# Grouped attention in a two-part transformer kernel: first scores inside the last tile of values, two halves of weights made beside late units, first sum of squares behind a column

## The chip, the cores and the metric

The kernel runs on one core of one Trainium2 chip. The metric is the time of one execution on the device in microseconds (us), lower is better; the median of several executions is given. Besides the DMA engines the core has TensorE (PE, matmuls and weight loads), VectorE (DVE), ScalarE (ACT), GpSimd (POOL, idle here) and SyncE (SP, which issues the DMAs). Each engine works through its own instructions in the order written, and they wait for each other through counting semaphores.

## The reference

Two transformer layers (differential attention, then grouped attention, each between two feed-forward halves), followed by two layers of a second kind. The change touches the grouped attention of the second layer, which is computed for the 256 positions of the main sequence (`ctx_out` is false there); keys and values also cover the 256 context positions:

```python
GA_HEAD_DIM = 128; GA_HEADS = 8; GA_KV_HEADS = 2
def gqa_axial_mixer(h, hc, w_in, q_norm, k_norm, w_out, ctx_out):
    q, k, v = project(h)        # one projection, q and k normed per head (rmsnorm over 128)
    qc, kc, vc = project(hc)
    q, k = apply_rope(q, cos, sin), apply_rope(k, cos, sin)
    k_all = jnp.concatenate([kc, k], axis=1)
    v_all = jnp.concatenate([vc, v], axis=1)
    # grouped_attend per block of 128 queries:
    s = jnp.einsum('blhgd,bkhd->bhglk', q, k) * scale
    p = jax.nn.softmax(s, axis=-1)
    o = jnp.einsum('bhglk,bkhd->blhgd', p, v)
    return o @ w_out
```

## The kernel before

All of it is one program with an order written out by hand for every engine. Weights stream through a ring of four slots of 1 MB; one slot holds two halves (128x1024). Before TensorE uses a half, ScalarE makes its high part (`high`, L1329) and VectorE its low part (`low`, L1942), and a product is three matmuls: high x high, high x low, low x high (L461 to L463, in the tiles of values L788 to L790). Only three halves have room at a time: when one is used up, ScalarE's `used()` waits for that and makes the one three further on; VectorE's `lows(n)` makes the low parts behind it. A low part that is done also lets SyncE load the next ring slot.

The grouped attention is the branch for the fifth of six sub-layers (`sub == 4`). Its stretch in the profile runs from about 1492 to 1621 us:

1. **Columns.** `first_columns` makes three columns (two key heads, 512 wide, and the first query head); seven more follow by `project(1, S)`. Per column ScalarE copies the bank to `mix` (L1666) and its squares to `sq` (L1667); TensorE sums the squares with a matmul against ones (`head_sum`, L1047, two instructions each); ScalarE makes the inverse root (`head_root`), VectorE scales (`ga_norm`, L2185), TensorE swaps pairs (`turn_head`, L802) and VectorE rotates (`ga_rope`: L2170, L2174, L2179). In the loop over t, `head_sum(t - 2)` stands behind the column of t, and for t = 2, which has no column, `head_sum(0)` stands by itself ahead of the first `project`.
2. **Values.** `values(4, ...)`: four tiles of 128 tokens, eight chunks of three matmuls each. Behind tile t stand `head_sum(8 + t)` for t < 2 and `turn_head(6 + t)`. ScalarE evacuates each tile (`v_tile`, L1685); after the fourth it has made two highs, and VectorE makes two lows behind the last rotation.
3. **Units.** `softmax_units`: 16 units, one for each head and each block of 128 queries. TensorE: `scores` (L1075), `turn` (four transposes, L822), `blend` (probabilities times values, L835). VectorE: maximum (L2199, L2208), reciprocal and scaling (L2213, L2220). ScalarE: exponential (L1543), copy of the turned block (L1552) and, each second unit, two copies of the head's output (L1697, L1698). TensorE's order is scores(0), scores(1), and then for each u: scores(u + 2), turn(u), blend(u - 1). ScalarE's is exponential(u), copy(u - 1), output(u - 2). VectorE's is maximum(u + 1), probabilities(u), with maximum(0) ahead of all.
4. **Output.** `project_out(S)`: eight columns; chunk k of the first waits for head k's low part (L2351).

Banks: columns and tiles of values alternate between `ps[0]` and `ps[1]`, rotations between `ps[2]` and `ps[3]`; scores of even units go to `ps[0]`, of odd units to `ps[2]`. Ahead of scores(0) TensorE waits until all rotations are read and the last tile of values is evacuated.

Of the kernel before, what the change touches and what calls it, by code (L numbers as in the profile page):

```python
# [15 lines left out]
KC = D // P  # L16
S = 256
TT = 2 * S
# [129 lines left out]
def program(nc, wk, x_in, cols_in, crow_in, tabs_in, htabs_in, trig_in, uk_in, uv_in, out):  # L148
    with ExitStack() as ctx:
# [302 lines left out]
        def _(pe):  # L452
# [322 lines left out]

            def values(toks, xh=u_hi, xl=u_lo, stride=TT, after=None, count=KC):

                nonlocal H, parts
                for t in range(toks):
                    if t == 0:  # L780
                        weights(H)
                    bank = bank_a()[:, 0:256]
                    for k in range(KC):
                        if t == 0 and k == 4:
                            weights(H + 1)
                        h, n = H + k // 4, k % 4 * 256
                        x_h, x_l = (x[:, k * stride + t * P:k * stride + (t + 1) * P] for x in (xh, xl))
                        mm(bank, x_h, half_hi(h, n, n + 256), start=k == 0, stop=False)  # L788
                        mm(bank, x_l, half_hi(h, n, n + 256), start=False, stop=False)  # L789
                        last = mm(bank, x_h, half_lo(h, n, n + 256), start=False, stop=k == KC - 1)  # L790
                        if t == toks - 1 and k % 4 == 3:
                            last.then_inc(half_done, 1)
                    if t < toks - 1:
                        last.then_inc(part_done, 1)
                        parts += 1
                    if after and t < count:
                        after(t)
                H += 2
# [5 lines left out]

            def softmax_units(specs, beside=None, free=None):
                nonlocal units, ofree
# [32 lines left out]
                N = len(specs)  # L839
                scores(0)  # L840
                scores(1)
                for u in range(N):
# [81 lines left out]
            for sub in range(6):  # L924
# [110 lines left out]
                else:  # L1035
# [19 lines left out]
                    def behind_values(t):  # L1055
                        if t < 2:
                            head_sum(8 + t)
                        turn_head(6 + t)

                    for t in range(2, 10):  # L1060
                        if t > 2:
                            project(1, S)
                        head_sum(t - 2)
                        if t >= 4:
                            turn_head(t - 4)
                    values(4, after=behind_values)
                    pe.wait_ge(v_free, v)
                    pe.wait_ge(a_free, a)
                    specs = []
                    for h, qt, klo in GA_UNITS:  # L1070
                        def scores(banks, h=h, qt=qt):
# [9 lines left out]
                            pt=lambda b, kt: mix[:, GA_PT + b * 512 + kt * P:GA_PT + b * 512 + (kt + 1) * P]))  # L1081
                    softmax_units(specs)
                    project_out(S)
# [222 lines left out]
        def _(act):  # L1306
# [180 lines left out]

            def value_tiles(toks, evacuate):
                nonlocal a, parts
                for t in range(toks):  # L1490
                    if t < toks - 1:
# [39 lines left out]

            def softmax_units(specs, ni, scale, heads_out, beside=None):
                nonlocal units, ofree
# [28 lines left out]
                for u in range(N + 2):  # L1562
                    if u < N:
                        exponentials(u)
                    if 1 <= u <= N:
                        turned(u - 1)
                    if u >= 2:
                        output(u - 2)
                    if beside:
                        beside(u)  # L1570
# [16 lines left out]
            for sub in range(6):  # L1587
# [73 lines left out]
                else:  # L1661
# [20 lines left out]
                    def v_tile(t, bank):  # L1682
                        if t in (1, 2):
                            head_root(7 + t)
                        return f(mix[:, GA_V_AT + t * 256:GA_V_AT + (t + 1) * 256], bank[:, 0:256], ACT.Copy)  # L1685
                    value_tiles(4, v_tile)
                    v += 10
# [8 lines left out]
                    def head_out(h, bank):  # L1696
                        f(u_hi[:, h * TT:h * TT + S], bank[:, 0:S], ACT.Copy)  # L1697
                        return f(uT[:, h * TT:h * TT + S], bank[:, 0:S], ACT.Copy)  # L1698
                    softmax_units(specs, 1, GA_HD ** -0.5, head_out)
                    y_tiles(sub, S)  # L1700
# [183 lines left out]
        def _(dve):  # L1884
# [301 lines left out]

            def softmax_units(specs, ni, scale, mix_lambda=False, beside=None, ahead=True):

# [32 lines left out]

                maxima(0)
                for u in range(N):
                    if ahead and u + 1 < N:
                        maxima(u + 1)
                    probabilities(u)
                    if not ahead and u + 1 < N:
                        maxima(u + 1)
# [25 lines left out]
            for sub in range(6):  # L2254
# [62 lines left out]
                else:  # L2317
# [16 lines left out]
                    for t in range(2, 10):  # L2334
                        lows(1)
                        ga_norm(t - 2)
                        if t >= 4:
                            ga_rope(t - 4)
                    for t in range(4):
                        if t < 2:  # L2340
                            ga_norm(8 + t)
                        ga_rope(6 + t)
                        if t == 3:
                            lows(2)
                    specs = [(lambda b, i: ps[2 * b][:, :], None,
                              lambda b: [mix[:, GA_PROB + b * 512:GA_PROB + (b + 1) * 512]]) for _ in GA_UNITS]
                    softmax_units(specs, 1, GA_HD ** -0.5)
                    for h in range(GA_HEADS):
# [524 lines left out]
```

## Time and profile before

| What | Value |
|---|---|
| time, median of 3 runs | 2539.0 us (2536.47 to 2540.21) |
| the profiled execution's own time | 2546.11 us |
| its span | 2544.3 us |
| TensorE busy with matmuls | 2441.0 us (96%) |
| TensorE weight loads (beside the matmuls) | 2104.3 us (83%) |
| VectorE busy | 1585.5 us (62%) |
| ScalarE busy | 1069.5 us (42%) |
| DMA | 348.77 MB, mean 137 GB/s |
| mean granted TensorE clock | 0.991 of full speed |

The profile is of one execution. Times in it are counted from the start of the span. In the timeline a row gives the start, the duration, the engine, the line of the kernel, the operation, what it writes and reads, and in brackets how long its engine sat idle before it and what ended that. The ends of matmuls are modelled; their starts are the better measure.

### The profile page before, as it was taken

The page shows a single profiled execution, that of the slowest core. Times are in us where ns is not written, and L with a number is a line of the kernel's source. Part 1 is how long each engine was busy: PE and PEld are TensorE (multiplying, and loading weights), DVE is VectorE, ACT ScalarE, POOL GpSimd, SP SyncE. Part 2 cuts the span into 40 slices and gives each one's busy share as a digit, 9 for nine tenths or more (in the row PEclk, how much of TensorE's full clock was granted, in tenths as well). Part 3 has the DMA queues.
Part 4 walks back from the last instruction along what each step waited for, and adds up shares of the span by engine and source line. Part 5 has one row for each costly group of instructions (what it writes and reads, how often), then busy time and mean ns, then how long its engine had stood idle before and what let it go on. Part 6 is the DMA issues. An engine that isn't in the chain of part 4 may idle for free.

```text
span 2544.3 us, 36416 instructions
## 1 busy us (share of the span) xinstructions
PE 2441.0 (96%) x14732; PEld 2104.3 (83%) x14732; DVE 1585.5 (62%) x2825; ACT 1069.5 (42%) x1877; POOL 0.2 (0%) x4
## 2 busy tenths in 40 slices
PE   8999999999889999999999989899899999999998
PEld 4888888866588888888888877899898988999887
DVE  7767766366567776377623366555665867666757
ACT  4222225355542222252222256544545555455563
POOL 0000000000000000000000000000000000000000
PEclk9999999999999999999999999999999999999999
DMA  6554451201125544215422211355443533434422
GB/s 266 193 199 184 182 194 54 100 34 50 50 68 201 198 186 195 99 63 202 183 99 100 100 66 67 123 185 188 142 174 121 179 116 133 158 137 162 149 101 84
DMA packets 48697, 348.77 MB, mean 137 GB/s; under 512 B 5393, under 2 KB 5521, under 8 KB 6801
## 3 DMA queue, kind: packets, MB, share of 16 engines
q1 hardware_dynamic: 48530, 346.44, 36.9%
q8 instruction: 118, 1.93, 0.3%
q14 instruction: 49, 0.40, 0.0%
HBM read 345.36 MB, written 1.05 MB: 136 GB/s over the span
## 4 chain that ended last, share of the span: by engine, by line
PE 89%; DVE 6%; ACT 3%; issue 1%; DMA 1%; SPq 0%; DVEq 0%; ACTq 0%
PE ps L461 25%; PE ps L462 24%; PE ps L463 24%; DVE w_lo L1942 2%; PE ps L788 1%; PE ps L790 1%; PE ps L789 1%; ACT w_hi L1329 1%; PE ps L835 1%; PE ps L965 1%; PE ps L665 1%; PE ps L991 1%; DMA hT<-in_x 1%; PE ps L822 1%; PE ps L615 1%
## 5 line engine op out<-in xcount | busy, mean ns | idle before, releaser
L1329 ACT ACTIVATE w_hi<-ring 128x1024 fp32r<-128x1024 f32 x504 | 533.5, 1060 | 1158.0 <-PE ps L463 1077.8
L1942 DVE TENSOR_TENSOR w_lo<-ring,w_hi 128x1024 fp32r<-128x1024 f32 x504 | 615.7, 1223 | 541.8 <-ACT w_hi L1329 539.1
L461 PE MATMUL ps<-u_hi,w_hi 128*128 128x512 f32 (+1 forms) x1856 | 664.4, 358 | 36.9 <-DVE u_lo L1990 20.4
L462 PE MATMUL ps<-u_lo,w_hi 128*128 128x512 f32 (+1 forms) x1856 | 654.8, 353 | 0.0
L463 PE MATMUL ps<-u_hi,w_lo 128*128 128x512 f32 (+1 forms) x1856 | 653.7, 352 | 0.0
L461 PEld LDWEIGHTS ps<-u_hi,w_hi 128*128 128x128 f32 x1856 | 353.4, 190 | 93.7 <-issue 29.1
L462 PEld LDWEIGHTS ps<-u_lo,w_hi 128*128 128x128 f32 x1856 | 353.3, 190 | 48.2 <-issue 0.5
L463 PEld LDWEIGHTS ps<-u_hi,w_lo 128*128 128x128 f32 x1856 | 353.2, 190 | 48.0
L461 PE MATMUL ps<-uh,w_hi 128*128 128x256 f32 x1184 | 340.6, 288 | 10.3 <-DVE ul L2378 5.6
L1930 DVE CUSTOM_DVE_ANT_0 waste<-ring,condb,cols 128x1024 f32<-128x1024 f32 x272 | 336.8, 1278 | 10.5 <-ACT condb L1578 7.8
L462 PE MATMUL ps<-ul,w_hi 128*128 128x256 f32 x1184 | 329.8, 279 | 0.0
L463 PE MATMUL ps<-uh,w_lo 128*128 128x256 f32 x1184 | 329.7, 278 | 0.0
L461 PE MATMUL ps<-h_hi,w_hi 128*128 128x512 f32 (+1 forms) x776 | 271.7, 350 | 3.5 <-DVE h_lo L2099 3.5
L462 PE MATMUL ps<-h_lo,w_hi 128*128 128x512 f32 (+1 forms) x776 | 269.1, 347 | 0.0
L463 PE MATMUL ps<-h_hi,w_lo 128*128 128x512 f32 (+1 forms) x776 | 268.6, 346 | 0.0
L461 PEld LDWEIGHTS ps<-uh,w_hi 128*128 128x128 f32 x1184 | 223.2, 189 | 20.5 <-issue 16.3
L462 PEld LDWEIGHTS ps<-ul,w_hi 128*128 128x128 f32 x1184 | 223.1, 188 | 0.3
L463 PEld LDWEIGHTS ps<-uh,w_lo 128*128 128x128 f32 x1184 | 222.9, 188 | 0.0
L2113 DVE TENSOR_TENSOR hidden<-ps,hidden 128x512 f32<-128x512 f32 (+1 forms) x88 | 54.9, 624 | 197.7 <-PE ps L463 197.7
L461 PEld LDWEIGHTS ps<-h_hi,w_hi 128*128 128x128 f32 x776 | 145.7, 188 | 24.9 <-DVE w_lo L1942 4.2
L462 PEld LDWEIGHTS ps<-h_lo,w_hi 128*128 128x128 f32 x776 | 146.0, 188 | 19.7
L463 PEld LDWEIGHTS ps<-h_hi,w_lo 128*128 128x128 f32 x776 | 145.9, 188 | 18.7
(333 smaller groups left out, 2666.5 us busy)
## 6 DMA issues: line engine op xcount, KB each, us to landing
ring<-in_wk SPq DMA_DIRECT2D x324, 1024.0 KB, 4.8
hT<-in_x SPq DMA_DIRECT2D x1, 2048.0 KB, 16.1
htabs<-in_htabs SPq DMA_DIRECT2D x1, 1152.0 KB, 7.0
out_t<-uT SPq DMA_DIRECT2D x2, 512.0 KB, 2.7
trig<-in_trig SPq DMA_DIRECT2D x3, 256.0 KB, 7.2
wuk<-in_uk SPq DMA_DIRECT2D x2, 256.0 KB, 5.3
wuv<-in_uv SPq DMA_DIRECT2D x2, 256.0 KB, 5.8
cols<-in_cols SPq DMA_DIRECT2D x1, 302.5 KB, 2.9
```

Of the source, the lines that this page charges most:

```text
L461: mm(bank, hi, x_hi, start=first, stop=False, skip_group_check=skip)
L462: mm(bank, hi, x_lo, start=False, stop=False, skip_group_check=skip)
L463: return mm(bank, lo, x_hi, start=False, stop=last, skip_group_check=skip)
L615: last = mm(bankN[:, S:TT], tab("ones"), sq[:, c * TT + S:(c + 1) * TT], start=c == 0, stop=c == KC - 1)
L665: last = mm(bankN[:, 0:T], tab("ones"), src[:, c * stride:c * stride + T], start=c == 0, stop=c == KC - 1)
L788: mm(bank, x_h, half_hi(h, n, n + 256), start=k == 0, stop=False)
L789: mm(bank, x_l, half_hi(h, n, n + 256), start=False, stop=False)
L790: last = mm(bank, x_h, half_lo(h, n, n + 256), start=False, stop=k == KC - 1)
L1329: f(half_hi(K, 0, HALF), ringed(n, K % 2 * HALF, (K % 2 + 1) * HALF), ACT.Copy).then_inc(whi_ready, 1)
L1930: last = nc.vector.tensor_tensor_reduce(waste[:, c * D:(c + 1) * D], ringed(slot, t * D, (t + 1) * D), condb[:, c * D:(c + 1) * D], 1.0, c ...
L1942: tt(half_lo(K, 0, HALF), ringed(HALF_SLOT[K], K % 2 * HALF, (K % 2 + 1) * HALF), half_hi(K, 0, HALF).bitcast(F32), ALU.subtract).then_inc ...
L2113: tt(h, bankV[v % 2][:, 0:T], h, ALU.mult).then_inc(v_free, 1)
```

## The change

Four edits, all in the grouped attention.

- **TensorE, first sum of squares.** `head_sum(0)` moves from ahead of the first `project` column to behind it, just ahead of `head_sum(1)`.
- **TensorE, first scores.** scores(0) is issued in the middle of the last tile of values, ahead of its fifth chunk, after a wait for the third tile's evacuation. scores(1) is issued behind the last rotation, after a wait that all rotations but the last are read. The wait for the last tile's evacuation moves to turn(0).
- **VectorE and ScalarE, order.** VectorE takes maximum(0) ahead of the last rotation (`ga_rope(9)`), and probabilities(0) ahead of maximum(1). ScalarE takes exponential(0) ahead of the evacuation of the last tile of values.
- **Halves.** The two highs behind the tiles of values and the two lows behind the last rotation go; in their place `beside(8)` and `beside(13)` of the units each have one high on ScalarE (after exponential(u), copy(u - 1) and output(u - 2)) and one low on VectorE (after maximum(u + 1) and probabilities(u)).

```diff
 values (TensorE)
+                        if t == toks - 1 and k == 4 and amid:
+                            amid()
 softmax_units (TensorE)
-                scores(0)
-                scores(1)
+                if not begun:
+                    scores(0)
+                    scores(1)
 grouped attention (TensorE)
                         turn_head(6 + t)
+                        if t == 3:
+                            pe.wait_ge(v_free, v - 1)
+                            specs[1]["scores"](ps[2:4]).then_inc(s_full, 1)
+                    def first_scores():
+                        pe.wait_ge(a_free, first + 13)
+                        specs[0]["scores"](ps[0:2]).then_inc(s_full, 1)
                     for t in range(2, 10):
                         if t > 2:
                             project(1, S)
-                        head_sum(t - 2)
+                            if t == 3:
+                                head_sum(0)
+                            head_sum(t - 2)
                         if t >= 4:
                             turn_head(t - 4)
-                    values(4, after=behind_values)
-                    pe.wait_ge(v_free, v)
-                    pe.wait_ge(a_free, a)
...
-                    softmax_units(specs)
+                    values(4, after=behind_values, amid=first_scores)
+                    softmax_units(specs, None, (a_free, a), True)
 softmax_units (ScalarE)
                     if u < N:
                         exponentials(u)
+                    if u == 0 and between:
+                        between()
 grouped attention (ScalarE)
-                    value_tiles(4, v_tile)
+                    value_tiles(4, v_tile, 3)
+                    def last_values():
+                        nonlocal a, H
+                        H += 2
+                        act.wait_ge(half_done, H)
+                        v_tile(3, bankA[a % 2]).then_inc(a_free, 1)
+                        a += 1
+                    def ga_beside(u):
+                        if u in (8, 13):
+                            high()
...
-                    softmax_units(specs, 1, GA_HD ** -0.5, head_out)
+                    softmax_units(specs, 1, GA_HD ** -0.5, head_out, ga_beside, last_values)
 softmax_units (VectorE)
                 maxima(0)
+                if between:
+                    between()
                 for u in range(N):
-                    if ahead and u + 1 < N:
+                    first = ahead and not (u == 0 and between)
+                    if first and u + 1 < N:
                         maxima(u + 1)
                     probabilities(u)
-                    if not ahead and u + 1 < N:
+                    if not first and u + 1 < N:
                         maxima(u + 1)
 grouped attention (VectorE)
-                    for t in range(4):
+                    for t in range(3):
                         if t < 2:
                             ga_norm(8 + t)
                         ga_rope(6 + t)
-                        if t == 3:
-                            lows(2)
+                    def ga_beside(u):
+                        if u in (8, 13):
+                            lows(1)
-                    softmax_units(specs, 1, GA_HD ** -0.5)
+                    softmax_units(specs, 1, GA_HD ** -0.5, beside=ga_beside, between=lambda: ga_rope(9))
```

## Rows read from the trace of the kernel before

**Rows 1.** The page, chain that ended last: shares of the span by engine.
```profile
PE 89%; DVE 6%; ACT 3%; issue 1%; DMA 1%; SPq 0%; DVEq 0%; ACTq 0%
```
**Rows 2.** Timeline around the first sums of squares (TensorE, ScalarE): start, duration, what.
```profile
1518.26 1.12 PE L1047 MATMUL ps<-sq,tabs 128*128 128x512 f32 x2 [1.42 <-ACT sq L1667]
1519.52 0.61 ACT L1667 ACTIVATE sq<-ps 128x512 f32<-128x512 f32 x1
1520.27 0.36 PE L461 MATMUL ps<-u_hi,w_hi 128*128 128x256 f32 x1 [0.89 <-ACT sq L1667]
1523.07 1.02 PE L1047 MATMUL ps<-sq,tabs 128*128 128x512 f32 x2
1526.76 0.59 PE L1047 MATMUL ps<-sq,tabs 128*128 128x256 f32 x2
```
**Rows 3.** Timeline, TensorE: first instructions after idles of about 3 us.
```profile
687.82 0.47 PE L461 MATMUL ps<-u_hi,w_hi 128*128 128x512 f32 x1 [3.29 <-DVE w_lo L1942]
1509.15 0.55 PE L461 MATMUL ps<-u_hi,w_hi 128*128 128x256 f32 x1 [2.81 <-DVE u_lo L1990]
1830.08 5.25 PE L665 MATMUL ps<-sq,tabs 128*128 128x256 f32 x16 [3.35 <-ACT sq L1343]
```
**Rows 4.** Stretches behind them and a full one: length, busy us (count) by engine, PEclk, DMA.
```profile
687.82:691.00 3.18, 3.18 (x14) 2.63 (x15) 2.49 (x3) 2.02 (x4) 0.00 (x0) 1.00 0.77 268
1509.15:1512.30 3.15, 3.15 (x15) 3.15 (x16) 3.15 (x9) 2.02 (x5) 0.00 (x0) 0.50 0.00 0
1830.00:1834.00 4.00, 3.92 (x11) 3.25 (x12) 4.00 (x12) 2.73 (x7) 0.00 (x0) 0.60 0.00 0
1603.00:1620.00 17.00, 17.00 (x143) 16.89 (x142) 8.69 (x10) 10.28 (x19) 0.00 (x0) 1.00 0.52 188
```
**Rows 5.** Timeline, end of the values and first units, all engines.
```profile
1556.72 0.37 ACT L1685 ACTIVATE mix<-ps 128x256 f32<-128x256 f32 x1
1557.50 0.28 PE L788 MATMUL ps<-w_hi,u_hi 128*128 128x256 f32 x1
1557.70 1.06 ACT L1329 ACTIVATE w_hi<-ring 128x1024 fp32r<-128x1024 f32 x1 [0.62 <-PE ps L790]
1558.87 0.59 PE L802 MATMUL ps<-mix,tabs 128*128 128x256 f32 x2
1559.57 0.42 DVE L2170 TENSOR_TENSOR mix<-ps,trig 128x256 f32<-128x256 f32 x1
1560.49 1.96 PE L1075 MATMUL ps<-mix 128*128 128x512 f32 x4 [1.03 <-DVE mix L2170]
1560.70 2.35 DVE L1942 TENSOR_TENSOR w_lo<-ring,w_hi 128x1024 fp32r<-128x1024 f32 x2
1562.97 0.68 DVE L2199 TENSOR_REDUCE small<-ps 128x1 f32<-128x512 f32 x1
1563.88 0.69 ACT L1543 ACTIVATE mix<-ps,small 128x512 f32<-128x512 f32 x1 [3.48 <-DVE small L2208]
1564.71 1.12 PE L1075 MATMUL ps<-mix 128*128 128x512 f32 x2 [2.26 <-ACT mix L1543]
1568.78 1.02 PE L1075 MATMUL ps<-mix 128*128 128x512 f32 x2
```
**Rows 6.** Timeline, late units, all engines.
```profile
1590.69 1.02 PE L1075 MATMUL ps<-mix 128*128 128x512 f32 x2
1592.74 0.49 DVE L2220 TENSOR_SCALAR mix<-mix,small 128x512 f32<-128x512 f32 x1
1592.88 1.02 PE L1075 MATMUL ps<-mix 128*128 128x512 f32 x2
1593.63 0.69 ACT L1543 ACTIVATE mix<-ps,small 128x512 f32<-128x512 f32 x1
1593.94 0.69 DVE L2199 TENSOR_REDUCE small<-ps 128x1 f32<-128x512 f32 x1 [0.72 <-PE ps L1075]
1595.47 0.66 PE L822 MATMUL ps<-tabs,mix 128*128 128x128 f32 x4 [0.23 <-DVE mix L2220]
```

## What the change will do: prediction

> **What bounds the kernel now.** I read the page's chain of waits first: TensorE carries 89% of the time that set the end [rows 1]. So the change is worth what it takes from or adds to TensorE's own line of work: its idle times, its added instructions, and its clock. Nothing else counts unless it comes back as one of these. The timeline of the grouped attention then shows where TensorE stands still: 1.42 us ahead of the first sum of squares and 0.89 us behind it [rows 2]; 1.03 us behind the last rotation and 2.26 us ahead of scores(2) [rows 5]. From there on its work is without a gap: scores start 2.19 us apart (1590.69, 1592.88) [rows 6], which is 0.86 for scores, 0.44 for four transposes and 0.89 for the blend. Only the last units wait for VectorE again, 0.23 us [rows 6]. So some 5.8 us of idle is all there is, 0.23% of the span.
>
> **Part 1, the first sum of squares: adds 0.9 us, and perhaps more.** Behind the third column TensorE stops at 1516.84 (1518.26 less 1.42 of idle). Sum 0 waits for the first squares. It runs from 1518.26, and the next column starts at 1520.27, released by the second tile's squares, 1519.52 + 0.61 = 1520.13 [rows 2]. That is the bank the column needs; the sum has no part in it. With the sum moved behind the column, the column still starts at 1520.27, since nothing on ScalarE ahead of that point changes. The sum was hidden in the wait and now stands in TensorE's gapless work. Its price: a column alone takes 1523.07 - 1520.27 = 2.80 us, a column with a 512-wide sum 1526.76 - 1523.07 = 3.69 [rows 2], so 0.89. What waits for the sum? head_root(0), now about 2.6 us later, with the next high behind it on ScalarE; the following columns have their halves and banks a column ahead, so I count nothing for it (if that cover were gone, up to the 0.9 us by which ScalarE falls behind).
>
> **The clock after the longer idle.** The idle there becomes one stretch of 1520.27 - 1516.84 = 3.43 us. What such a stretch does is seen elsewhere: after 2.81 us the granted clock was 0.50 (the level of 1.2 GHz) and TensorE made 15 matmuls in 3.15 us, 0.21 each, where the full clock (2.4 GHz) makes 143 in 17.00, 0.119 each; after 3.35 us it was 0.60 over 4 us; after 3.29 us it stayed at 1.00 [rows 3, 4]. The pattern of 2.81 us with a clock at the half level stands three more times in the trace; idles of 2.88 and 2.75 us left it at full. So a fall is likelier than not, but not sure; I give it 6 in 10. Its price is bounded by 0 and by 15 x (0.21 - 0.119) = 1.4 us; I take 1.2, as the slow stretch may begin within the idle. The two short idles of before (1.42 and 0.89) left the clock full.
>
> The Trainium skill ("TensorE: Matmul & The Clock Gate", Part 1) says that the throttled clock is the default which activity releases, and that the outcome varies from run to run, since the activity monitor runs free of the kernel's start. By it the same idle may cost nothing in one execution and the full price in the next; this case's trace agrees, with falls after 2.81 and none after 3.29 us.
>
> **Part 2, the earlier start of the units: saves 2.7 us.** Worked out in the times of before:
> - The fifth chunk of the last tile starts at 1557.50; the evacuation that scores(0) waits for ends at 1556.72 + 0.37 = 1557.09 [rows 5]. No wait; 0.4 us is its cover. Scores take 0.86 wherever they stand, so the values end at 1558.87 + 0.86 = 1559.73, the rotation (0.43, half of a 512-wide sum) at 1560.16, scores(1) at 1561.02.
> - VectorE is free of rotation 8 at about 1559.5 and takes maximum(0) at once, instead of at 1562.97. There it stood behind rotation 9 and the two lows, 2.35 us [rows 5]. From maximum to exponential is 1563.88 - 1562.97 = 0.91 with one maximum and its scaling; so exponential(0) starts at 1560.4, and from it to scores(2) is 1564.71 - 1563.88 = 0.83: scores(2) at 1561.24, where it was 1564.71 [rows 5].
> - Rotation 9 on VectorE runs 1560.4 to 1561.5, probabilities(0) follows, turn(0) at 1562.2. Maximum(1) stands behind them: 1562.1, exponential(1) 1563.0, scores(3) 1563.8. This is what is late next: 1.2 us of idle. Then turn(1) 1564.7, blend(0) 1565.1, scores(4) at 1566.0, where it was 1568.78 [rows 5]. From here the 2.19 us beat holds.
> The gain is 2.7 us. The last tile's evacuation, now behind exponential(0), ends at 1561.5, ahead of turn(0), which is queued behind it on TensorE: 0.7 us of cover. The interruption of a tile of values may cost up to 0.2 us (a change of matmul kind); I leave it in the range: 2.4 to 2.8.
>
> **Part 3, the two halves beside units 8 and 13: add 0.5 and 1.9 us.** They were on the path too, and 2.35 us of the gain above is theirs; now they come back at another place. A low takes 1.17 us of VectorE and waits for its high, 1.06 us [rows 5]. In the beat VectorE idles about 0.8 us in a unit (0.72 ahead of a maximum [rows 6]), and its probabilities come 0.5 us before the turn that needs them: 1592.74 + 0.54 = 1593.28 against scores at 1592.88 + 0.86 = 1593.74 [rows 6]. So 1.3 us can be hidden.
> - Unit 8: ScalarE comes to the high right behind copy(7), and VectorE waits some 0.65 us for it, then 1.13. Sum 1.8, less 1.3: turn(9) is 0.5 us late.
> - Unit 13: by ScalarE's order the high stands behind output(11). That output ends where exponential(14) starts, 1593.63. VectorE is done with probabilities(13) at 1592.74 + 0.40 = 1593.14 and finds no high until 1593.63 + 1.1 = 1594.73. The low ends at 1595.9, so maximum(15), due at 1593.94, starts 1.95 us late, and probabilities(14) stand behind it; the turn(14) that waits for them had no slack left (0.23 us of idle already) [rows 6]. It moves from 1595.47 to about 1597.5. A little is caught up behind it: 1.9 us.
> Bounds: 0 to 1.2 for unit 8, 0.8 (only the low itself over the slack) to 2.3 for unit 13. Exponential(14) is behind the high as well, but ends ahead of the delayed probabilities. The halves are needed by the second and third output columns, 2.8 and 5.6 us behind the units: no wait there. SyncE's next ring load is issued behind the first of these lows, some 20 us later than before; its data are for the sixth output column, so nothing waits for it.
>
> **The sum.** 0.9 - 2.7 + 0.5 + 1.9 = +0.6 us; with the fall of the clock +1.8. The profiled execution took 2546.11 us, 1.8 over its span and 7.1 over the median; none of the terms depends on the difference, so I put the sum on the median: 2539.0 + 1.8 = 2540.8 us.
>
> **The rivals.**
> - *No fall of the clock*: the same sum with 0, 2539.6 us. For it: 3.29 us at full clock [rows 3, 4].
> - *The halves are hidden.* If ScalarE's high is done in time at both units, part 3 costs about 0.2 and the change gives -2.7 + 0.9 + 0.2: 2537.4 us. For it: ScalarE is busy 42%. Against: its order, output(11) ahead of the high.
> - *The early scores don't bring it.* If the evacuation of the third tile is late or the first exponential is held up, so that the units start only 1 us earlier, then the gain is 1.0 and the result 2542.5 us. For it: only 0.4 us of cover. It is also the case in which the change doesn't do what it says.
> - *Slower by more than 0.2%: the clock falls again and again.* Mechanism: all idles behind the changed stretch come at another moment, and the new idle of over 2 us at turn(14) is one more. Price 1.4 each. It decides the sign from three more falls on: 1.8 + 3 x 1.4 = +6.0, 2545 us. Against: before has the same idles and its falls already.
>
> **How the numbers follow.** What a measurement of this kernel can tell from no change is about 0.2%, 5 us. Chances: forecast with the fall 0.42, without it 0.27, hidden halves 0.12, late start 0.08, more falls 0.05; 0.06 is left for what I don't see. Only the fifth leaves the 0.2% upwards, with a part of what is left: slower 0.07, faster 0.03, same 0.90. The range: downwards to the hidden halves with the spread of the runs of before, which is 1.9 us to either side, 2536.5; upwards to the late start with the same spread, 2544.5.
>
> **What the profile would show.** Part 1: one idle of 3.4 us ahead of the fourth column and no sum in it; PEclk under 1 in the stretch behind it or not. Part 2: L1075 within the last tile of values, L2199 directly behind L2179, from the fifth chunk of the last tile to scores(4) 8.5 us, where it was 11.3 (1557.50 to 1568.78). Part 3: L1942 twice within the units, turn(9) with some 0.5 us and turn(14) with over 2 us of idle, released by L2220. The prediction is wrong if the fourth column starts before 1520, if the lows cost nothing, or if the columns behind the moved sum wait.

## The result, and the profile after

The changed kernel takes 2542.02 us (median of 21 executions) beside 2537.0 us of the kernel before in as many: ratio 1.0018, 95% interval 1.0010 to 1.0025. By the ratio that is 4.6 us slower, at the edge of the 0.2% that the prediction called no change. The forecast was 1.8 us slower, 2540.8 us, with a range up to 2544.5 us; it stood on a median of 2539.0 us from 3 executions of the kernel before, which over 21 is 2537.0.

The two profiled executions can't be compared by their spans (2538.4 us after, 2544.3 before). The first row below is the start of the first columns' second part, ahead of every edit; in the profile of before it stands at 1509.15 [rows 3]. So 9.0 us of the difference lie in code that the change does not touch. What follows is therefore measured from this row on. Timeline of the changed kernel around the first sums:

```profile
1500.17 0.55 PE L461 MATMUL ps<-u_hi,w_hi 128*128 128x256 f32 x1 [2.81 <-DVE u_lo L2016]
1511.38 0.55 PE L461 MATMUL ps<-u_hi,w_hi 128*128 128x256 f32 x1 [3.42 <-ACT sq L1681]
1516.64 2.18 PE L1050 MATMUL ps<-sq,tabs 128*128 128x512 f32 x4
1521.38 0.59 PE L1050 MATMUL ps<-sq,tabs 128*128 128x256 f32 x2
```

and its stretches behind the idle (columns as in rows 4):

```profile
1511.38:1514.50 3.12, 3.12 (x14) 3.12 (x15) 1.36 (x2) 1.35 (x3) 0.00 (x0) 0.50 0.74 291
1514.50:1518.00 3.50, 3.50 (x14) 2.85 (x14) 0.00 (x0) 0.01 (x1) 0.00 (x0) 0.61 0.76 290
```

The fourth column starts where it did (11.21 us behind the first row; before 1520.27 - 1509.15 = 11.12 [rows 2, 3]). The idle is one of 3.42 us, and the column takes 5.26 us instead of 2.80, at a granted clock of 0.50, the 1.2 GHz level. The third sum, which is common to both, stands at 21.21 us; before it was 1526.76 - 1509.15 = 17.61 [rows 2, 3]. That is 3.6 us lost: 0.9 the sum itself, 2.7 the clock.

The start of the units, which answers to [rows 5]:

```profile
1552.02 1.02 PE L1086 MATMUL ps<-mix 128*128 128x512 f32 x2
1554.02 0.68 DVE L2225 TENSOR_REDUCE small<-ps 128x1 f32<-128x512 f32 x1
1554.92 0.69 ACT L1555 ACTIVATE mix<-ps,small 128x512 f32<-128x512 f32 x1 [3.32 <-DVE small L2234]
1558.46 1.12 PE L1086 MATMUL ps<-mix 128*128 128x512 f32 x2 [0.94 <-ACT mix L1555]
1560.75 1.02 PE L1086 MATMUL ps<-mix 128*128 128x512 f32 x2
```

scores(0) stand in the last tile of values, the first maximum comes 2.0 us behind their start, and scores(4) 8.73 us. Counted from the same place, the end of the tile's fourth chunk, scores(4) came after 11.28 us before [rows 5]: 2.55 us won. The two halves, and the late units of [rows 6]:

```profile
1573.70 1.05 ACT L1341 ACTIVATE w_hi<-ring 128x1024 fp32r<-128x1024 f32 x1
1574.78 1.23 DVE L1968 TENSOR_TENSOR w_lo<-ring,w_hi 128x1024 fp32r<-128x1024 f32 x1 [0.54 <-ACT w_hi L1341]
1577.44 0.66 PE L824 MATMUL ps<-tabs,mix 128*128 128x128 f32 x4 [0.33 <-DVE mix L2246]
...
1585.40 1.02 PE L1086 MATMUL ps<-mix 128*128 128x512 f32 x2
1585.88 0.38 ACT L1724 ACTIVATE uT<-ps 128x256 f32<-128x256 f32 x1
1586.14 1.06 ACT L1341 ACTIVATE w_hi<-ring 128x1024 fp32r<-128x1024 f32 x1
1587.24 1.23 DVE L1968 TENSOR_TENSOR w_lo<-ring,w_hi 128x1024 fp32r<-128x1024 f32 x1 [1.49 <-ACT w_hi L1341]
1589.90 0.66 PE L824 MATMUL ps<-tabs,mix 128*128 128x128 f32 x4 [2.15 <-DVE mix L2246]
1593.60 0.36 PE L461 MATMUL ps<-u_hi,w_hi 128*128 128x256 f32 x1
```

Each row of VectorE's low (L1968) names ScalarE's high (L1341) as what it waited for, the second high stands right behind the copies of a head's output (L1724), and each late turn (L824) names VectorE's probabilities. Turn(9) is 0.5 us late (the scores around it start 2.74 us apart instead of 2.19); from scores(15) to the first output column it is 8.20 us, 6.29 before (1592.88 [rows 6] to 1599.17): 1.9 us.

### The profile page after: what moved, and what is told of

Its sections match the earlier page's. It is cut to its first block, busy times and chain, and to the rows that moved or that the text cites. A ratio compares the mean times of both kernels' runs of the same rounds, so it can differ in the third digit from the quotient of the medians.

```text
span 2538.4 us, 36415 instructions
## 1 busy us (share of the span) xinstructions
PE 2435.2 (96%) x14732; PEld 2103.2 (83%) x14732; DVE 1584.3 (62%) x2825; ACT 1069.1 (42%) x1877; POOL 0.2 (0%) x4
## 4 chain that ended last, share of the span: by engine, by line
PE 88%; DVE 6%; ACT 4%; issue 2%; DMA 1%; DVEq 0%; SPq 0%; ACTq 0%
PE ps L461 25%; PE ps L462 24%; PE ps L463 24%; DVE w_lo L1968 2%; PE ps L790 1%; ACT w_hi L1341 1%; PE ps L791 1%; PE ps L792 1%; PE ps L968 1%; PE ps L837 1%; PE ps L994 1%; DMA ring<-in_wk 1%; PE ps L824 1%; PE ps L615 1%; PE ps L1268 1%
## 5 line engine op out<-in xcount | busy, mean ns | idle before, releaser
L1341 ACT ACTIVATE w_hi<-ring 128x1024 fp32r<-128x1024 f32 x504 | 533.5, 1060 | 1146.9 <-PE ps L463 1069.5
L1968 DVE TENSOR_TENSOR w_lo<-ring,w_hi 128x1024 fp32r<-128x1024 f32 x504 | 615.7, 1223 | 537.6 <-ACT w_hi L1341 535.0
L461 PE MATMUL ps<-uh,w_hi 128*128 128x256 f32 x1184 | 340.5, 288 | 10.2 <-DVE ul L2408 5.6
```

The costliest lines, as they stand in the source:

```text
L461: mm(bank, hi, x_hi, start=first, stop=False, skip_group_check=skip)
L1341: f(half_hi(K, 0, HALF), ringed(n, K % 2 * HALF, (K % 2 + 1) * HALF), ACT.Copy).then_inc(whi_ready, 1)
L1968: tt(half_lo(K, 0, HALF), ringed(HALF_SLOT[K], K % 2 * HALF, (K % 2 + 1) * HALF), half_hi(K, 0, HALF).bitcast(F32), ALU.subtract).then_inc ...
```

## The experiments

All stretches are taken from the timelines in the same way: A from the start of the first columns' second part to the third sum; B from there to the last rotation; C from there to the first output column. Line numbers differ from kernel to kernel, the names of the tiles do not. All us:

```
kernel                                   A      B      C    A+B+C  output column    ratio (95%)
                                                                   to next half
before                                 17.61  32.11  40.30  90.02     37.23
c1 before again                        19.34  32.21  40.32  91.87     37.07   0.9998 (0.9984 to 1.0012)
after                                  21.21  32.91  39.31  93.43     37.33   1.0018 (1.0010 to 1.0025)
c2 after again                         20.86  32.91  39.32  93.09     37.21   1.0012 (1.0003 to 1.0021)
e1 sum ahead                           20.57  33.12  39.30  92.99     37.23   1.0007 (0.9996 to 1.0017)
e2 sum alone                           21.19  32.11  40.31  93.61     37.21   1.0018 (1.0009 to 1.0026)
e3 after, idle broken                  18.57  33.02  40.77  92.36     37.90   1.0033 (1.0021 to 1.0045)
e10 e2, idle broken                    18.31  32.01  41.48  91.80     37.99   1.0006 (0.9994 to 1.0018)
e7 halves alone                        17.72  32.11  41.02  90.85     36.97   1.0021 (1.0010 to 1.0032)
e8 scores alone                        17.53  33.02  41.34  91.89     37.61   1.0020 (1.0010 to 1.0029)
e4 sum ahead, halves apart             17.55  33.02  36.85  87.42     38.47   1.0011 (1.0002 to 1.0019)
e9 the same, other units               17.60  33.12  36.84  87.56     38.44   0.9996 (0.9982 to 1.0009)
e11 after, halves apart                20.87  33.02  36.84  90.73     38.49   1.0009 (0.9999 to 1.0020)
```

The column to the right of the sum runs from the first output column to the first column of the next feed-forward half. B is 0.8 to 1.0 us longer where scores(0) stand in it, and C shorter by as much.

**The first sum.** e1 takes this part back:

```diff
                         if t > 2:
                             project(1, S)
-                            if t == 3:
-                                head_sum(0)
-                            head_sum(t - 2)
+                        head_sum(t - 2)
```

> The changed kernel with head_sum(0) back ahead of the first project column; all else as changed. Theory (the moved sum costs 0.9 us of TensorE work and 2.6 us of half clock, as the profile after shows): the fourth column starts where it did and takes 2.8 us instead of 5.26, the granted clock behind it is 1.00, and the stretch from the start of the first columns' second part to the first output column is 93.4 - 3.5 = 89.9 us; the time is some 0.1 us below the kernel before (ratio 0.999 to 1.000). Rival (the price lies in the later units, not in the sum): the stretch stays above 92 us and the ratio at 1.0018.

A was 20.57 us and not 17.6, so this trace did not decide by itself: the half clock that had followed the 2.81 us idle at the start of A lasted longer (sum 0 came 1.3 us later than before), and it came back. The stretch of 92.99 us is what the rival had asked for, the ratio is between the two. Stretch of e1's fourth column:

```profile
1513.71:1518.15 4.44, 4.44 (x24) 4.44 (x25) 2.12 (x3) 2.56 (x5) 0.00 (x0) 0.62 0.68 266
```

What the order of before does on average is only seen over several kernels that have it. e2 is the reverse, the kernel before with only this move (the same diff, the other way):

> The kernel before with nothing changed but head_sum(0), which moves behind the fourth column. Theory: an idle of 3.4 us ahead of the fourth column, then half clock in most executions; the stretch from the first columns' second part to the first output column is 90.0 + 3.5 = 93.5 us where the clock falls and 90.9 where it does not; ratio 1.0010 to 1.0015. Rival (only the 0.9 us of the sum counts, the clock falls elsewhere anyway): ratio 1.0004 or less.

Its fourth column, at the half level throughout (24 matmuls in 5.19 us):

```profile
1514.11:1519.30 5.19, 5.19 (x24) 5.19 (x25) 1.36 (x2) 1.34 (x3) 0.00 (x0) 0.50 0.81 295
```

A is 21.19, the ratio 1.0018, above the expected 1.0015: this move alone loses as much as the whole change, and the rest of the change comes out near nothing. Then the long idle is taken away and the move kept, in the changed kernel (e3) and in e2 (e10):

```diff
+                    pe.wait_ge(a_free, first + 1)
+                    mm(ps[6][:, 0:TT], tab("ones"), sq[:, GA_K:GA_K + TT], start=True, stop=True)
                     for t in range(2, 10):
```

> The changed kernel with an extra copy of head_sum(0) where it stood before (its result is overwritten by the real one and nobody is told), so that the idle ahead of the fourth column is broken in two and the moved sum stays where it is. Theory (the long idle brings the half clock): no fall of the clock, the fourth column takes 2.8 us, the stretch is 93.4 - 2.6 = 90.8 us, ratio about 1.0003 to 1.0006. Rival (the half clock comes from something else than the length of this idle): the fourth column takes 5.3 us as in the changed kernel, ratio 1.0018.

> The kernel before with the first sum moved behind the fourth column (as e2) and an unused copy of it left in its old place, so that the idle there is 1.4 and 0.9 us long and not 3.4. Theory (the moved sum costs 0.9 us as work, the rest of e2's loss is the clock behind the long idle): from the start of the first columns' second part to the third sum 18.5 us where it was 17.6, and 21.2 in e2; ratio 1.0003 to 1.0007. Rival (the long idle is not what matters): 21 us, ratio 1.0018 as in e2.

A was 18.57 and 18.31 us, 0.7 to 1.0 above 17.6: with the idle broken the move costs what the sum costs as work, and the clock stays. The rival of each falls for this stretch. But e3's stretch is 92.36 us where 90.8 was expected, and its ratio, 1.0033, is far above the expected 1.0006. A part is seen in its trace: the idle of 2.14 us ahead of turn(14) was followed by a low clock, which made C 1.5 us longer:

```profile
1589.60:1594.76 5.16, 5.16 (x32) 5.16 (x33) 3.00 (x9) 2.02 (x6) 0.00 (x0) 0.67 0.00 0
```

e10's C is 1.2 us longer as well: the clock is low behind the idle of 2.26 us ahead of its scores(2), which left it full in the kernel before. Its ratio, 1.0006, is as expected.

```profile
1563.74:1567.50 3.76, 3.34 (x9) 1.63 (x10) 2.35 (x8) 2.41 (x7) 0.00 (x0) 0.73 0.47 196
```

**How much is the execution.** The two kernels once more, without an edit:

> The kernel before, unchanged, in another execution. In the traces so far stretches that no edit touches differ: matmuls 0.114 or 0.118 us apart at full clock (512 wide: 0.229 or 0.233), and half clock at other idles. Theory (this is a matter of the execution, not of the edits): this trace differs from the first one of the same kernel by several us outside the grouped attention as well, the stretch from the first columns' second part to the first output column is 90.0 us or up to 1.5 us more where the clock falls, and the ratio holds 1. Rival (the edits bring the differences about): this trace repeats the first one within 1 us in every stretch.

> The changed kernel, unchanged, in another execution. Theory: the idle of 3.42 us stands ahead of the fourth column again and half clock behind it, 1 to 2.7 us dear; units 8 and 13 again cost 0.5 and 1.9 us; the stretch is 91 to 95 us. Rival (the half clock of the first trace was an accident): the fourth column takes 2.8 us and the stretch is 90.8 us.

c1's start of A stands at 1503.61, 5.5 us earlier than in the first trace of the same kernel, so the rival (every stretch repeats within 1 us) falls. Its B and C repeat to 0.1 us, but A is 19.34: with idles of 1.41 and 0.88 us around sum 0 the clock was low there too. Stretch of c1's fourth column:

```profile
1514.83:1519.27 4.44, 4.44 (x25) 4.44 (x26) 2.12 (x3) 2.56 (x5) 0.00 (x0) 0.62 0.79 280
```

c2 repeats the changed kernel (20.86, 32.91, 39.32). So with the sum moved and the idle whole A was 20.86 to 21.21 in four traces of four (after, c2, e2, e11); with the sum ahead it was 17.53 to 17.72 in five of seven and 19.34 and 20.57 in the two others, mean 18.3. The mean difference is 2.8 us: 0.9 of work, 1.9 of clock. Of e1's A 1.3 us were lost ahead of sum 0, behind another idle; counted from the start of the fourth column, the difference is 3.0 us (10.0 beside 7.0), 2.1 of it clock.

**The units.** e7 has only the halves moved (no early scores, no change of order), e8 only the early scores and the order, with both highs behind exponential(0) and both lows behind the last rotation:

```diff
 e7, against the kernel before (VectorE; on ScalarE the highs move alike)
-                        if t == 3:
-                            lows(2)
...
-                    softmax_units(specs, 1, GA_HD ** -0.5)
+                    softmax_units(specs, 1, GA_HD ** -0.5, beside=ga_beside)
 e8, against e1 (VectorE; on ScalarE both highs stand ahead of the last evacuation)
...
-                    softmax_units(specs, 1, GA_HD ** -0.5, beside=ga_beside, between=lambda: ga_rope(9))
+                    softmax_units(specs, 1, GA_HD ** -0.5, between=rope_and_lows)
```

> The kernel before with one part of the change alone: the two halves are made beside units 8 and 13 instead of behind the values; first scores, first sum and the order of the first unit stay. Theory: the units begin 1.4 us earlier (the two lows no longer stand ahead of the first maximum, but the scores now do), and the two units give back 0.5 and 1.9 us; the stretch is 91.0 us, ratio 1.0002 to 1.0008. Rival (what stood on the path were the late scores, not the lows): the start gains under 0.5 us, the stretch is 92 us.

> The changed kernel with head_sum(0) ahead of the columns and with the two halves made where they were before: the highs behind exponential(0), the lows behind the last rotation, ahead of probabilities(0). So of the change only the early scores and the first unit's order are left. Theory (the two lows, 2.3 us, are most of what the early start gained, and early scores alone move the wait): scores(4) comes within 0.5 us of where it stood before, counted from the last tile's fifth chunk, 11.3 us; the units run on without an idle of over 0.3 us; the stretch is 90.0 to 90.4 us. Rival (the early scores are the gain, the lows were hidden): scores(4) comes 2 us earlier, the stretch is 88 us.

e7: C is 0.7 us longer than before; 2.4 of cost (its end, 8.19 us from scores(15), is that of the changed kernel) less 1.7 won at the start. The expected 91.0 came out as 90.85, and the rival falls; but the ratio, 1.0021, is far above the expected 1.0002 to 1.0008 (see below). e8: two rows tell it, the first turn waiting 2.81 us and scores(3) behind it at a low clock:

```profile
1558.64 0.66 PE L824 MATMUL ps<-tabs,mix 128*128 128x128 f32 x4 [2.81 <-DVE mix L2239]
```
```profile
1560.24:1564.20 3.96, 3.96 (x15) 2.82 (x15) 2.03 (x6) 2.19 (x6) 0.00 (x0) 0.57 0.19 79
```

At full clock that stretch takes 2.29 us (1558.46 to 1560.75 in the changed kernel), so 1.7 us of e8's 91.89 are the clock's and 90.2 is left, as expected. scores(4) come 13.2 us behind scores(0), 11.5 without the clock's part, where it was 11.28. So early scores without the lows out of the way gain nothing, they only move the wait to turn(0). The two lows and the late scores stood beside each other on the way to the first maximum.

**Where the halves may stand.** e4 has the sum ahead and moves high and low to units without a head's output, the low one unit later; e9 does so at other units, e11 with the moved sum.

```diff
 e4 (e9: 2, 6 and 3, 7)
-                        if u in (8, 13):
+                        if u in (4, 8):
                             high()
-                        if u in (8, 13):
+                        if u in (5, 9):
                             lows(1)
```

> The changed kernel with head_sum(0) ahead of the columns again, and the two halves beside other units: the highs on ScalarE beside units 4 and 8 (no head's output there), the lows on VectorE one unit later, beside 5 and 9. Theory (a low costs only where it waits for its high, and 1.13 us fit into 0.8 us of idle and 0.5 us of slack): units beat at 2.19 us throughout, no idle of TensorE over 0.3 us until the end, the stretch is 90.0 - 2.55 = 87.5 us; ratio 0.9985 to 0.9995. Rival (any half among the units costs what it takes, 1 us each): the stretch is 89.5 us or more.

> As e4 (first sum ahead of the columns, early scores), with the highs beside units 2 and 6 and the lows beside 3 and 7. Theory (apart by one unit, a half is hidden wherever it stands in the beat): no idle of TensorE over 0.3 us from scores(4) to the last units, from the last rotation to the first output column 36.9 us where it was 40.3; the stretch is 87.4 us, up to 3 us more where the clock falls; ratio 0.999, and e4's 1.0011 was what unchanged stretches did in its executions. Rival (something outside the stretch answers to the early scores and takes 4 us): the stretch is 87.4 us again and the ratio again 1.001.

> The changed kernel, the first sum behind the fourth column as it has it, with nothing changed but the two halves: highs beside units 4 and 8, lows beside 5 and 9. Beside e9 it shows the moved sum. Theory: to the third sum 21.1 us (17.6 without the move), from the last rotation to the first output column 36.9 us; the stretch is 91.0 us, the ratio 1.0010 above e9's. Rival (the moved sum is hidden when the units start early): the stretch is 88 us and the ratio that of e9.

C is 36.85, 36.84 and 36.84 us: the two halves cost nothing. TensorE's one idle from scores(4) to the output, in e4:

```profile
1584.32 0.66 PE L824 MATMUL ps<-tabs,mix 128*128 128x128 f32 x4 [0.24 <-DVE mix L2243]
```

And e11's A is 20.87, that is, the move costs the same there; its ratio is 0.0013 above e9's, where 0.0010 was expected; the two intervals overlap. So the stretch of e4 and e9 is 2.5 us shorter than before, as expected. Yet e4's ratio was 1.0011 where 0.9985 to 0.9995 was expected, and e9's 0.9996. The column of the table to the right of the sum shows where the gain went: from the first output column to the first column of the next feed-forward half all three take 38.4 to 38.5 us, where before, its repetition, after and its repetition take 37.1 to 37.3. In e9 the sums of squares and the columns behind the idles of 2.75 and 2.88 us run at

```profile
1618.17:1624.78 6.61, 6.61 (x16) 5.00 (x16) 3.77 (x12) 2.83 (x7) 0.00 (x0) 0.55 0.00 0
1627.66:1631.26 3.60, 3.60 (x18) 3.60 (x19) 3.60 (x10) 2.19 (x6) 0.00 (x0) 0.55 0.02 5
```

and in the kernel before, in the same place, at

```profile
1628.12:1633.52 5.40, 5.40 (x16) 3.88 (x16) 3.77 (x12) 2.84 (x7) 0.00 (x0) 0.68 0.00 0
1636.40:1640.00 3.60, 3.60 (x28) 3.51 (x29) 3.60 (x10) 2.19 (x6) 0.00 (x0) 1.00 0.02 5
```

The sums take 1.2 us longer, and in 3.60 us of the next columns 18 matmuls are done instead of 28, worth 10 x 0.117 = 1.2 us. Together 2.4 of the 2.5 us are given back, in three traces of three (e4 and e11 have 18 matmuls there as well). But the short stretch isn't needed for it: behind the same idle of 2.88 us e3, e10 and e8 have 17 or 18 matmuls at 0.50 to 0.55 too, and their stretches are not shorter, while the seven others have 28 at 1.00. So the loss is seen; that the earlier end of the stretch brings it about is not shown.

**The clock of every execution.** The mean granted clock is on record for each execution, also for those without a trace. If nothing but the clock differed, 0.001 less of it would be some 0.001 x 2540 = 2.5 us. This is a rough estimate, since TensorE doesn't work all the time. Means over the executions of a kernel, beside those of the kernel before in the same group; all us but the clocks:

```
          clock    before's   by the clock   by the ratio (95%)
e1        0.9906   0.9911          1.4        1.8 (-1.0 to 4.3)
e2        0.9896   0.9911          3.8        4.6 (2.3 to 6.6)
e3        0.9880   0.9911          8.0        8.4 (5.3 to 11.4)
e4        0.9896   0.9911          3.8        2.8 (0.5 to 4.8)
c1        0.9901   0.9905          1.1       -0.5 (-4.1 to 3.0)
c2        0.9888   0.9905          4.3        3.0 (0.8 to 5.3)
e7        0.9882   0.9905          5.8        5.3 (2.5 to 8.1)
e8        0.9886   0.9905          4.8        5.1 (2.5 to 7.4)
e9        0.9901   0.9903          0.4       -1.0 (-4.6 to 2.3)
e10       0.9891   0.9903          3.0        1.5 (-1.5 to 4.6)
e11       0.9885   0.9903          4.6        2.3 (-0.3 to 5.1)
```

What a kernel works more or less comes on top: for e2 3.8 + 0.9 = 4.7 us, beside 4.6 by its ratio. So the slower kernels had less clock on average, by about what they lost. For e7 it also says why its trace shows so little: the profiled execution took 2539.51 us at a clock of 0.991, 5.1 us below the kernel's median of 2544.62.

**The clock itself.** If half clock behind idles is what costs, TensorE must be kept busy in them. e12 is e9 with matmuls of constants into banks that the next real matmul overwrites:

```diff
+            def keep_warm(to, times=5):
+                for _ in range(times):
+                    mm(to, tab("ones"), tabs[:, 0:S], start=True, stop=True)
 two_columns, ahead of the first chunk
+                keep_warm(banks[0][:, 0:S])
 first_columns, ahead of the second part's first chunk
+                    if s:
+                        keep_warm(pair[0][:, S:TT])
 norm_term, ahead of the first sum of squares
+                    keep_warm(bankN[:, 0:S], 3)
```

> e9 with small matmuls of constants (128x256, plain fp32, nobody reads them) issued into banks that are about to be overwritten, where TensorE otherwise stands idle for 2.75 to 2.88 us: five ahead of the first columns' second part and of each pair of first columns, three ahead of the sums of squares of a whole stream. The computation is the same. Theory (what e4, e9 and e11 gave back between the output and the next feed-forward half is half clock behind those idles): PEclk is 1.00 behind the output's sums, from the first output column to the first column of the next half 35.5 to 36 us where it was 37.2 in the kernel before and 38.4 in e9; the half clock at the seven other idles of this kind goes as well, 1.3 to 2.6 us each; ratio 0.994 to 0.997. Rival (the idles are not what sets the clock there, or the added matmuls delay what they precede): 37.2 us or more, ratio 0.999 or above.

It takes 2528.16 us beside 2539.46 of the kernel before, ratio 0.9960 (0.9946 to 0.9974), where e9 had 0.9996. The page's first line, and the three stretches of the grouped attention and behind it:

```profile
PE 2449.0 (97%) x14824; PEld 2110.1 (84%) x14824; DVE 1584.8 (63%) x2825; ACT 1069.6 (42%) x1877; POOL 0.2 (0%) x4
```
```profile
1497.45:1500.60 3.15, 3.15 (x25) 3.05 (x25) 3.15 (x9) 2.04 (x5) 0.00 (x0) 1.00 0.02 5
1612.82:1617.80 4.98, 4.98 (x16) 2.65 (x17) 3.86 (x12) 2.83 (x7) 0.00 (x0) 1.00 0.00 0
1620.77:1624.37 3.60, 3.60 (x27) 3.49 (x28) 3.60 (x10) 2.19 (x6) 0.00 (x0) 1.00 0.00 0
```

92 more matmul instructions in ten places, and 25 real ones in 3.15 us behind the idle where before had 15 [rows 4]. A is 16.72 us, 0.8 under the best of the others. From the output to the next half it is 36.8 us (1583.96 to 1620.77), 1.6 less than e9, though not the 35.5 to 36 expected: the sums still follow ScalarE's squares, which come 0.67 us apart, each waiting for VectorE's `hT` (1613.02, 1613.69, 1614.36). The mean granted clock was 0.995 to 0.997 in the six executions and 0.989 to 0.992 in those of the kernel before; by the estimate above 0.005 more is 13 us, and 10.2 were measured by the ratio.

## Why the prediction was right, and where it was not

**Part 1, the sum as work: right.** 0.9 us was forecast; e3 and e10 show 1.0 and 0.7. That the column starts at the same moment, since the bank and not the sum holds it, shows in all traces (10.9 to 11.2 us behind the start of A, but for e1 with its low clock). The columns behind it did not wait.

**Part 1, the clock: the mechanism was right, the term was mis-sized.** The step that failed is the price "bounded by 0 and by 15 x (0.21 - 0.119) = 1.4 us; I take 1.2". It took one slow stretch of 3.15 us as the longest. Behind the 3.42 us idle the half clock lasted through the whole fourth column and into the sums: 2.7 us in the profile after, in e2 as well. The chance of 6 in 10 was perhaps too low as well: the clock fell four times of four, which 6 in 10 gives in 0.6^4 = 0.13 of cases. On the other side the text said that the two short idles of before leave the clock full; c1 and e1 show that they don't always. One reading was wrong too: the text said that an idle of 2.75 us leaves the clock full, but of the two in the trace of before the one ahead of the sums at 1628.12 is followed by 0.68. The errors partly cancel: against the mean of the order of before the clock costs 1.9 us, not 2.7.

The Trainium skill ("TensorE: Matmul & The Clock Gate", Part 1) says that the outcome differs from execution to execution, since the monitor runs free of the kernel. The traces agree: one kernel has A 17.61 and, in c1, 19.34, and full clock or 0.56 behind the same idle of 3.3 us (last section). For the long idle, on the other hand, four traces agree within 0.4 us.

**Part 2: right.** 2.7 us forecast, 2.55 measured (2.4 to 2.8 was the range), by the path named: maximum(0) free of the two lows. e7 and e8 add what it is made of: the lows out of the way win 1.7 us alone, the early scores alone nothing, both together 2.55.

**Part 3: right.** 0.5 and 1.9 us forecast, 0.5 and 1.9 measured, by the mechanism named: the low waits for its high, the high stands behind output(11), and turn(14) has no slack. The same low costs nothing one unit behind its high and in a unit that still has its slack (e4, e9, e11), as 1.13 us fit into the 0.8 of idle and 0.5 of slack. Whether a low alone at unit 13, where the text gave at least 0.8, would cost that much was not run.

**The sum.** With 0.9 + 2.7 of part 1 instead of 0.9 + 1.2, the stretch becomes 3.4 us longer, which is what the profile after shows (93.43 against 90.02), and 2.6 us on the mean of before's order (0.9 + 1.9 - 2.55 + 0.5 + 1.9 = 2.65). In c2's executions the loss was 3.0 us (0.8 to 5.3), in the first ones 4.6 (2.5 to 6.3). Both hold 2.65. So the loss first measured is two and a half times the forecast of 1.8, and the class "no change" and the range held by some luck: the range's upper end was set by the late start, not by a dearer clock, and it stood on a median 2 us higher. The idle of 2.15 us at turn(14), whose effect on the clock the text had in its rival only, brought a low clock in one of the five traces that have it (e3, 1.5 us), 0.3 us on average.

**The rivals.** "The halves are hidden" and "the early scores don't bring it" fell, "no fall of the clock" too. "The clock falls again and again" named the right mechanism; in both traces of the changed kernel it does not show (full clock at turn(14) and in the next half), but e3, e4, e8, e9, e10 and e11 have such falls, and in e4, e9 and e11 they eat a true gain.

**Still open.** e3 (8.4 us by its ratio) and e7 (5.3) lose more than their traces explain. e3's trace has 1.5 us in C, 0.7 behind it and 1.3 in the columns of the next half (17 matmuls instead of 28); with the moved sum that is some 4.3 us. e7's explains 0.6. Over all their executions both had less clock, by 8.0 and 5.8 us of the estimate, so the clock is the likely cause; behind which idles it fell in those without a trace, and why more often than in the kernel before, is not shown. e4's trace comes out even, and its ratio says 2.8 us (0.5 to 4.8).

## What to carry to other kernels

An instruction that fills a wait costs nothing there and its full length elsewhere; before moving it, ask what it was breaking up, since one idle of 3.4 us cost two to three times what the moved work did. A pair of steps on two engines (here high and low) is hidden only if the second engine reaches it after the first is done: put them a unit apart, and never where the first engine has extra work in that unit. And a gain of 2 us ahead of idles of 2 to 3 us can be lost behind them: look at the granted clock there, and at its mean over many executions, before trusting one trace. Small matmuls without a reader, into a bank about to be overwritten, filled such idles and gave 0.4% here, more than all the rest.

## What the runs showed of the hardware

- The granted clock was at the half level behind an idle of 2.14 us (e3), behind a pair of 1.41 and 0.88 us (c1), and for more than one column behind 3.42 us (after, c2, e2, e11).
- The length of an idle doesn't decide alone. The idle of 3.28 or 3.29 us that was followed by full clock in the kernel before [rows 3, 4] stands ahead of the same instruction in all fourteen traces: the clock was full behind it in five (before, after, c2, e2, e3) and low in nine. One of these is the same kernel, c1:

```profile
679.25 0.77 PE L461 MATMUL ps<-u_hi,w_hi 128*128 128x512 f32 x1 [3.28 <-DVE w_lo L1942]
679.25:682.43 3.18, 3.17 (x8) 2.56 (x9) 2.49 (x3) 2.02 (x4) 0.00 (x0) 0.56 0.67 258
```

- At full granted clock the same matmuls have two paces. In one feed-forward stretch of equal code 681 matmuls were done in 80 us in the kernel before (0.1175 us each) and 709 in e1 (0.1128); the two kernels are equal there, and no wait shows in either:

```profile
1660.00:1740.00 80.00, 80.00 (x681) 80.00 (x681) 40.52 (x44) 34.21 (x43) 0.00 (x0) 1.00 0.54 186
```
```profile
1650.00:1730.00 80.00, 80.00 (x709) 80.00 (x708) 42.38 (x44) 34.81 (x44) 0.00 (x0) 1.00 0.54 196
```

The two traces of the kernel before differ in the same way elsewhere, 345 and 351 matmuls of 512 columns in the same 80 us:

```profile
140.00:220.00 80.00, 80.00 (x345) 64.79 (x344) 56.84 (x81) 19.33 (x23) 0.00 (x0) 1.00 0.50 194
```
```profile
140.00:220.00 80.00, 80.00 (x351) 65.66 (x350) 55.80 (x80) 18.36 (x22) 0.00 (x0) 1.00 0.52 202
```

From 60 to 380 us that adds up to 1379 and 1406 matmuls, 27 x 0.23 = 6.2 us between two executions of one kernel, more than the change was worth. This is the reason why the table goes by stretches and not by spans. What sets the pace is not known.
